# Four edits to a two-block layer: logits over four column strips, the gate exponentials ahead of the row copies, the first transfers in another order, and the first expert's second weights held until the first gathered rows are in

## The reference, cut to what matters

```python
mod = silu(c) @ ada_w + ada_b                 # 1024 x 6144, split in shift1, scale1, gate1, shift2, scale2, gate2
h   = rms_norm(x, norm1_g) * (1 + scale1) + shift1
z   = h @ w_in                                # then RWKV-7 time mix and stick-breaking attention, w_out
h2  = rms_norm(x, norm2_g) * (1 + scale2) + shift2
logits = h2 @ router_w + router_b             # 512 x 32
top_logit, top_idx = top_k(logits, 4); top_gate = softmax(top_logit)
out[token] = sum over its 4 experts e: top_gate * (swiglu(h2 @ w1[e] + b1[e]) @ w2[e] + b2[e])
```

## Time and profile before

| | |
|---|---|
| median of three runs | 2655.41 us (2650.86 to 2656.16) |
| the profiled execution | 2653.22 us, its span 2651.5 us |
| mean granted clock of TensorE in it | 0.964 of full |
| PE busy | 2513.9 us, 95% of the span |
| DVE, ACT, POOL busy | 38%, 15%, 7% |
| moved by transfers | 555.43 MB, mean 209 GB/s |

### The profile page before, as it was taken

One profiled execution on the slowest core, in us unless ns is written; L12 is line 12 of the kernel. 1 busy time (PEld: TensorE's weight loads), 2 busy tenths in 40 slices (PEclk: granted clock), 3 DMA queues, 4 the chain that ended last, 5 costly groups with the idle time before them and its releaser, 6 DMA issues.

```text
span 2651.5 us, 49064 instructions
## 1 busy us (share of the span) xinstructions
PE 2513.9 (95%) x20545; PEld 1407.8 (53%) x20545; DVE 1017.6 (38%) x2012; ACT 406.4 (15%) x797; POOL 196.3 (7%) x256
## 2 busy tenths in 40 slices
PE   4999989796999999999999999699999998999999
PEld 2444777654333344433333444345556544888888
DVE  5563655424322333333222332423145222455551
ACT  2411134412000000000000000101234201111100
POOL 0000000000111111111111111400000000000000
PEclk8999999897999999999999999799999999999999
DMA  7432000105899999999999999750200112121221
GB/s 273 154 127 95 3 2 1 66 0 230 358 421 422 422 422 422 421 422 422 422 422 422 422 422 387 261 184 33 95 33 32 33 32 64 64 96 64 88 66 54
DMA packets 143743, 555.43 MB, mean 209 GB/s; under 512 B 15760, under 2 KB 51632, under 8 KB 94240
## 3 DMA queue, kind: packets, MB, share of 16 engines
q1 hardware_dynamic: 127088, 515.22, 48.9%
q0 software_dynamic: 13984, 36.49, 3.8%
q10 hardware_dynamic: 2576, 2.36, 0.3%
HBM read 537.25 MB, written 16.78 MB: 209 GB/s over the span
## 4 chain that ended last, share of the span: by engine, by line
PE 91%; DVE 4%; ACT 2%; issue 1%; DMA 1%; POOL 1%; SPq 0%; DVEq 0%; ACTq 0%; POOLq 0%
PE psum L2491 25%; PE psum L2082 20%; PE psum L2507 12%; PE psum L2777 10%; PE psum L2806 5%; PE psum L2240 2%; PE psum L2412 2%; PE psum L2696 2%; PE psum L2673 1%; PE psum L2354 1%; PE psum L2380 1%; PE psum L2651 1%; PE psum L2661 1%; PE psum L2070 1%; DVE arena L1305 1%
## 5 line engine op out<-in xcount | busy, mean ns | idle before, releaser
L2491 PE MATMUL psum<-ring,arena 128*32 128x512 f32 x6144 | 668.0, 594 | 10.0 <-DVE arena L1680 6.6
L2491 PEld LDWEIGHTS psum<-ring,arena 128*32 128x32 f32 x6144 | 196.8, 110 | 452.9 <-issue 452.3
L2082 PE MATMUL psum<-hT,ring 128*128 128x512 f32 x752 | 341.4, 611 | 3.4 <-ACT hT L829 3.4
L2507 PE MATMUL psum<-ring,arena 128*32 128x256 f32 x6144 | 337.4, 379 | 2.1 <-DVE arena L1714 2.1
L2507 PEld LDWEIGHTS psum<-ring,arena 128*32 128x32 f32 x6144 | 200.1, 110 | 146.6 <-issue 20.8
L2082 PEld LDWEIGHTS psum<-hT,ring 128*128 128x128 f32 x752 | 145.2, 196 | 182.5 <-issue 181.0
L1680 DVE STREAM_TRANSPOSE arena<-arena 128x768 f32<-128x768 f32 x33 | 32.3, 979 | 512.9 <-PE psum L2491 512.8
L760 POOL DMA_INDIRECT arena<-h_rows,small x102 | 100.1, 981 | 1310.2 <-DVE small L1689 1263.0
L2777 PE MATMUL psum<-ring 128*128 128x256 f32 x704 | 159.1, 379 | 0.5 <-ACT arena L815 0.5
L1014 ACT ACTIVATE arena<-arena 128x768 f32<-128x768 f32 x32 | 27.0, 843 | 823.3 <-DVE arena L1700 823.3
L2777 PEld LDWEIGHTS psum<-ring 128*128 128x128 f32 x704 | 133.7, 190 | 19.1 <-ACT arena L815 0.9
(11 more groups left out here) (391 smaller groups left out, 2590.1 us busy)
## 6 DMA issues: line engine op xcount, KB each, us to landing
ring<-in_exp_w SPq DMA_DIRECT2D x384, 1024.0 KB, 14.3
ring<-in_w_in SPq DMA_DIRECT2D x15, 2048.0 KB, 7.8
ring<-in_ada_w SPq DMA_DIRECT2D x12, 2048.0 KB, 8.1
ring<-in_w_ffn_in SPq DMA_DIRECT2D x22, 1024.0 KB, 7.7
expert_rows<-arena POOLq DMA_DIRECT2D x128, 96.0 KB, 6.0
ring<-in_w_ffn_out SPq DMA_DIRECT2D x8, 1408.0 KB, 6.7
ring<-in_w_out SPq DMA_DIRECT2D x2, 2048.0 KB, 7.9
ring<-in_w_o SPq DMA_DIRECT2D x2, 2048.0 KB, 7.5
```

Of the source, the lines that this page charges most:

```text
L2082: ins = mm(dst, l, r, start=(i == 0), stop=(i == len(parts) - 1))
L2491: ins = mm(bank[s][q * SG:(q + 1) * SG, :], XG[:, k, s * SG:(s + 1) * SG], w[:, q], start=(k == 0), stop=(k == KD - 1))
L2507: ins = mm(bank[3 + s // 2][q * SG:(q + 1) * SG, (s % 2) * 256:(s % 2 + 1) * 256], aT2k[:, s, k // 2, k % 2, :], w2_slot(k)[:, q * 256:(q ...
```

## The change

1. *First transfers.* SP issues `vec` and the positions, then `ada` chunks 0 and 1, then `xT` and `cst`, then `ada` 2 and 3, then the three small matrices, then `lora`, `k` and the rest. DVE begins with `cond` and `ada(0)`, `ada(1)`, and computes the angles between `ada(1)` and `ada(2)`. ACT makes squares and root first and the sines after them. PE sums the first two `ada` chunks ahead of the squares.
2. *Logits.* `router_w[:, k, :]` (32 columns) becomes the loaded weight and 128 tokens of `hT` stream; the four token tiles write to the four strips of 32 partitions of one bank. The result is experts by tokens, so DVE copies it out (128x128), PE transposes it once, and one DVE instruction of 128x128 adds the bias.
3. *Gates.* ACT runs the exponentials before the eight copies of token rows.
4. *Pass count.* Two small instructions over the thresholds take the place of the chain of comparisons.
5. *Second weights.* SP waits for the first gather's 48 counts before it issues w2 of expert 0; B2, the loads of `n_pass` and w1 of expert 1 stand behind that wait in its stream.

```diff
-    keys += [("lg", t) for t in range(NT)] + [("ht", t, i) for t in range(NT) for i in range(2)]
+    keys += [("lg",), ("lgT",)] + [("ht", t, i) for t in range(NT) for i in range(2)]
...
         def _(sp):
-            sp.dma_start(cst[:, :], a["consts"]).then_inc(tables_in, 16)
             sp.dma_start(vec[:, :], a["vecs"]).then_inc(tables_in, 16)
-            sp.dma_start(xT[:, :, :], a["xT"]).then_inc(x_in, 16)
-            sp.dma_start(up_wa[0:64, :], a["decay_up"][0]).then_inc(up_in, 16)
-            sp.dma_start(up_wa[64:128, :], a["iclr_up"][0]).then_inc(up_in, 16)
-            sp.dma_start(up_g, a["gate_up"][0]).then_inc(up_in, 16)
-            sp.dma_start(u_pos[:, :], a["positions"]).then_inc(up_in, 16)
+            sp.dma_start(u_pos[:, :], a["positions"]).then_inc(tables_in, 16)
             for (kind, i), s, after in loads:
+                if (kind, i) == ("ada", 2):
+                    sp.dma_start(xT[:, :, :], a["xT"]).then_inc(x_in, 16)
+                    sp.dma_start(cst[:, :], a["consts"]).then_inc(x_in, 16)
+                elif (kind, i) == ("win", "lora"):
+                    sp.dma_start(up_wa[0:64, :], a["decay_up"][0]).then_inc(up_in, 16)
+                    sp.dma_start(up_wa[64:128, :], a["iclr_up"][0]).then_inc(up_in, 16)
+                    sp.dma_start(up_g, a["gate_up"][0]).then_inc(up_in, 16)
...
             load_w1(0, 0)
+            sp.wait_ge(rows_in, 16 * GROUPS)
             load_w2(0, 0)
...
-            act.wait_ge(x_in, 16)
-            act.wait_ge(tables_dve, 1)
-            act.activation(cos_sin[:, :, :, :].rearrange("p j t f -> p (j t f)"), trig[:, 0:256], ACT.Sin).then_inc(tables_act, 1)
+            act.wait_ge(x_in, 32)
             for k in range(KD):
                 square(k)
             root(0)
+            act.wait_ge(tables_dve, 2)
+            act.activation(cos_sin[:, :, :, :].rearrange("p j t f -> p (j t f)"), trig[:, 0:256], ACT.Sin).then_inc(tables_act, 1)
             scale_shift(0, 0)
...
             scale_shift(1, 24)
+            act.wait_ge(top_ready, 1)
+            act.activation(TOPG, TOPG, ACT.Exp).then_inc(eg_ready, 1)
             for t in range(NT):
                 for i in range(2):
                     take(("ht", t, i), h2_split[:, t, 4 * i:4 * i + 4], ACT.Copy,
...
             act.dma_start(h2_d.rearrange("(t p) n -> p t n", p=P), h2_tok).then_inc(h2_out, 16)
-            act.wait_ge(top_ready, 1)
-            act.activation(TOPG, TOPG, ACT.Exp).then_inc(eg_ready, 1)
...
-            for n in range(4):
-                ada(n)
+            ada(0)
+            ada(1)
+            angles()
+            ada(2)
+            ada(3)
...
-            for t in range(NT):
-                b = plan.bank(("lg", t))
-                dve.wait_ge(filled, plan.at["lg", t] + 1)
-                link_evac(dve.tensor_tensor(LG[:, t, :], bank[b][:, 0:EXPERTS], row("router_b"), ALU.add), ("lg", t))
+            dve.wait_ge(filled, plan.at["lg",] + 1)
+            dve.tensor_copy(logits_T, bank[plan.bank(("lg",))][:, 0:P]).then_inc(evac[plan.bank(("lg",))], 1)
+            dve.wait_ge(filled, plan.at["lgT",] + 1)
+            link_evac(dve.tensor_tensor(LG, bank[plan.bank(("lgT",))][:, 0:P].rearrange("p (t e) -> p t e", t=NT),
+                                        row("router_b")[:, None, :].to_broadcast([P, NT, EXPERTS]), ALU.add), ("lgT",))
...
-            link(dve.tensor_scalar(NPF[:, 1:2], NPF[:, 0:1], CAP + 0.5, 1.0, ALU.is_gt, ALU.add))
-            for n in range(2, MAX_PASS):
-                link(dve.scalar_tensor_tensor(out=NPF[:, 1:2], in0=NPF[:, 0:1], scalar=n * CAP + 0.5, in1=NPF[:, 1:2],
-                                              op0=ALU.is_gt, op1=ALU.add))
-            link(dve.tensor_scalar(NPF[:, 2:3], NPF[:, 1:2], float(EXPERTS), -1.0, ALU.mult, ALU.add))
+            link(dve.tensor_scalar(GTMP[:, 0:MAX_PASS - 1], const("iota", MAX_PASS)[:, 1:MAX_PASS], float(CAP), NPF[:, 0:1], ALU.mult, ALU.is_lt))
+            link(dve.tensor_reduce(NPF[:, 3:4], GTMP[:, 0:MAX_PASS - 1], AX.X, ALU.add))
+            dve.tensor_scalar(NPF[:, 1:2], NPF[:, 3:4], 1.0, None, ALU.add)
+            link(dve.tensor_scalar(NPF[:, 2:3], NPF[:, 3:4], float(EXPERTS), EXPERTS - 1.0, ALU.mult, ALU.add))
...
-            pe.wait_ge(tables_in, 32)
+            pe.wait_ge(x_in, 32)
+            sum_mod(0)
+            sum_mod(1)
             for k in range(KD):
                 sum_square(0, k)
-            for n in range(4):
-                sum_mod(n)
+            sum_mod(2)
+            sum_mod(3)
...
-            for t in range(NT):
-                b = plan.bank(("lg", t))
-                pe.wait_ge(evac[b], plan.turn(("lg", t)))
+            b = plan.bank(("lg",))
+            pe.wait_ge(evac[b], plan.turn(("lg",)))
             for k in range(KD):
                 pe.wait_ge(h_ready, KD + k + 1)
                 for t in range(NT):
-                    ins = mm(bank[plan.bank(("lg", t))][:, 0:EXPERTS], hT[:, k, t * P:(t + 1) * P], router_w[:, k, :],
+                    ins = mm(bank[b][t * EXPERTS:(t + 1) * EXPERTS, 0:P], router_w[:, k, :], hT[:, k, t * P:(t + 1) * P],
                              start=(k == 0), stop=(k == KD - 1))
-                    if k == KD - 1:
-                        ins.then_inc(filled, 1)
+            ins.then_inc(filled, 1)
+            tile_evacuated(pe, ("lg",))
+            turn(("lgT",), [logits_T])
```

More of the change, by code:

```diff
@@ L431, in program @@
         GATE_T = A(26)[0:EXPERTS, :]
+        logits_T = A(27)[:, 0:P]
         B1_ROWS = hflat[:, 0:T]
@@ L1273, in _ @@
             dve.wait_ge(tables_in, 32)
-            dve.wait_ge(up_in, 64)
-            link(dve.tensor_copy(small[:, 120:124], u_pos[:, :]))
-            ang, turns = trig[:, 128:256], trig[:, 256:384]
-            for t in range(NT):
-                ins = dve.tensor_scalar(ang[:, t * 32:(t + 1) * 32], const("inv_freq"), small[:, 120 + t:121 + t], None, ALU.mult)
-            link(ins)
-            link(dve.tensor_scalar(turns, ang, 1.0 / TURN, ROUNDER, ALU.mult, ALU.add))
-            link(dve.tensor_scalar(turns, turns, ROUNDER, None, ALU.subtract))
-            for part in TURN_PARTS:
-                link(dve.scalar_tensor_tensor(out=ang, in0=turns, scalar=-part, in1=ang, op0=ALU.mult, op1=ALU.add))
-            link(dve.tensor_scalar(ang, ang, PI_LOW, -PI_LOW, ALU.min, ALU.max))
-            link(dve.tensor_scalar(trig[:, 0:128], ang, TURN / 4, None, ALU.add))
-            link(dve.tensor_scalar(turns, trig[:, 0:128], TURN / 2, -TURN, ALU.is_gt, ALU.mult))
-            link(dve.tensor_tensor(trig[:, 0:128], trig[:, 0:128], turns, ALU.add))
-            dve.tensor_scalar(trig[:, 0:128], trig[:, 0:128], PI_LOW, -PI_LOW, ALU.min, ALU.max).then_inc(tables_dve, 1)
             dve.tensor_scalar(omka, vec[:, VEC_AT["k_a"]:VEC_AT["k_a"] + 4], -1.0, 1.0, ALU.mult, ALU.add)
@@ L1293, in _, with angles @@
             dve.tensor_tensor(cond, sigc, vec[:, VEC_AT["c"]:VEC_AT["c"] + KD], ALU.mult).then_inc(tables_dve, 1)
-            dve.wait_ge(tables_dve, 2)
+            dve.wait_ge(tables_dve, 1)
+            def angles():
+                dve.wait_ge(x_in, 32)
+                link(dve.tensor_copy(small[:, 120:124], u_pos[:, :]))
+                ang, turns = trig[:, 128:256], trig[:, 256:384]
+                for t in range(NT):
+                    ins = dve.tensor_scalar(ang[:, t * 32:(t + 1) * 32], const("inv_freq"), small[:, 120 + t:121 + t], None, ALU.mult)
+                link(ins)
+                link(dve.tensor_scalar(turns, ang, 1.0 / TURN, ROUNDER, ALU.mult, ALU.add))
+                link(dve.tensor_scalar(turns, turns, ROUNDER, None, ALU.subtract))
+                for part in TURN_PARTS:
+                    link(dve.scalar_tensor_tensor(out=ang, in0=turns, scalar=-part, in1=ang, op0=ALU.mult, op1=ALU.add))
+                link(dve.tensor_scalar(ang, ang, PI_LOW, -PI_LOW, ALU.min, ALU.max))
+                link(dve.tensor_scalar(trig[:, 0:128], ang, TURN / 4, None, ALU.add))
+                link(dve.tensor_scalar(turns, trig[:, 0:128], TURN / 2, -TURN, ALU.is_gt, ALU.mult))
+                link(dve.tensor_tensor(trig[:, 0:128], trig[:, 0:128], turns, ALU.add))
+                dve.tensor_scalar(trig[:, 0:128], trig[:, 0:128], PI_LOW, -PI_LOW, ALU.min, ALU.max).then_inc(tables_dve, 1)
             def ada(n):
@@ L2127, in gates @@
                 if c == 0:
-                    pe.wait_ge(up_in, 64)
+                    pe.wait_ge(up_in, 48)
                     pe.wait_ge(gates_lo, 2)
@@ L2184, in _ @@
             head_sum(0)
-            pe.wait_ge(up_in, 80)
+            pe.wait_ge(up_in, 64)
             pe.wait_ge(inverse_ready, 1)
```

4 lines of the change are left out of this document (1 added, 3 removed).

## The result

| | before | after |
|---|---|---|
| median | 2650.86 us (five runs, 2648.08 to 2656.16) | 2637.10 us (five runs, 2634.99 to 2639.03) |
| ratio after to before | | 0.9942, interval 0.993 to 0.9955 |
| profiled execution, its span | 2653.22, 2651.5 us | 2637.1, 2635.1 us |
| mean granted clock of TensorE | 0.964 | 0.969 |

Two runs of before, taken beside the five of after, joined the three of the forecast. Of the two profiled executions the span is 16.4 us shorter. Three instants divide that difference: the first reciprocal (S), the reciprocal after the first block's residual (R), which begins the routing, and the first expert's first product (F).

A forecast was written before the change was run, and what follows sets the result against it. PE was taken as the bound, with 91% of the chain. Gains of 2.9 (start) and 9.9 (routing) sum to 12.8: 2653.2 becomes 2640.4, and the median, 2.2 above the profiled execution, 2642.5 us; main case 2637 to 2648.

The forecast's parts named there:

- everything from the first product on shifts by the start's 2.9 us: Sign to look for in the trace: all work from PE's first product onward comes 2.9 us earlier.
- Part 1, the start: First transfers reordered: DVE begins sooner, first reciprocal at 40.0 instead of 42.85 us; gain 2.9, bounds 2.3 and 3.6.
- "28.5" and "28.8": At the start, two estimates in us of when the transfers needed before ada(2) have landed; 28.2 was taken.
- Rival (d): The start gives nothing, ada(2) or the angles coming 3 us late: 2645.5 us; inside the main case of chance 0.84.
- Part 2, the logits: Router logits over four strips at 0.11 us per instruction, PE ending at 625.6; first maximum at 626.8, 7.0 us earlier.
- Rival (a): In the logits the strips do not overlap, loads or the four streams serialise: 2649.5 us; chance 0.07.
- Part 3, gates and rows: Exponentials before row copies: store issued at 634.0 instead of 640.28, landed at 641.3; pass count 637.2, 11.2 us earlier.
- Rival (c): PE stays at 1.2 GHz through the counts: gather at 646.1, 2644.5 us; inside the main case of chance 0.84.
- Part 4, the gather: From store landing and POOL's load of the pass number to the gather: at 644.1, 9.9 us earlier, bounds 8 and 11.
- Part 5, the held w2: Holding expert 0's w2 until the first gather leaves 2 us of backlog in the expert loop, cost 0, cover 3 us.
- rival (b): Transfers give out in the expert loop, hidden waits for w1: mild 2647 us, chance 0.06; slow 2659 us, chance 0.03.
- rival (e): Despite held w2 the store takes 9.4 us: gather near 646, 2644.5 us; inside the main case of chance 0.84.

The follow-up runs named there:

- a4_small_late: The changed kernel with the three small matrices (decay_up, iclr_up, gate_up) issued behind the k chunk; 2637.12 us, ratio 0.995 (0.9934 to 0.9965).
- b1_exp_late: The changed kernel with the exponentials again behind the row copies and the store; one execution, gather at R + 30.5, F at R + 37.6, no total time given.

## Where the prediction failed, and where it held

**The steps that failed.** The direction, the stage that carries the gain and what must be held for it came as forecast. The terms of the sum did not. The start was put at 2.9 us and measured 1.3 in the profiled pair, 0.8 over all executions. The routing was put at 9.9 and measured 12.35, above its bounds of 8 to 11. And "everything from the first product on shifts by the start's 2.9 us" put the stretch between S and R at nothing; it was 2.3 us shorter in this pair, by a scatter that reaches 9.8 us over all executions. Together that is 15.9 us at the first expert's product against 12.8: the start gave 1.6 less, the routing 2.45 more and the stretch between them 2.3 more.

**How much of the total was luck.** The medians differ by 13.8 us, close to the forecast 12.9, since the error of the start and that of the routing have opposite signs. Against the 2655.41 us from which the forecast was made the measured median is 18.3 lower; 4.55 of that is only that the median of before fell to 2650.86 with two more runs. The stated 2637 to 2648 does not follow from its terms either: 2641 less 4.5 and 2645 plus 0.8 give 2636.5 to 2646.

**Part 1, the start: mis-sized.** The step that failed is "28.5" and "28.8", the arrival of `ada(2)`, and with it `ada(3)`. Both came from a rate or an arrival of the old order, and took it that bytes cost the same in any order. `ada(0)` began at 10.88 for 9, the angles at 23.91 for 22.8, `ada(2)` at 29.33 for 28.2. `ada(3)` waited 0.32 more where the forecast had no wait, which `a4_small_late` puts down to the small matrices; S was 41.56 for 40.0. Rival (d), the start gives nothing, which lay inside the main case, was nearer to the truth than the 2.9. That the order of large and small rows at the front causes the lower rate is argued from the windows of the first 10 us, not shown: no run changed that alone.

**Part 2, the logits: right, and slightly better.** Taken at 0.11 us each, measured 0.70/8 = 0.088 in the last eight; ended 0.7 us behind ACT's last tile; the first maximum 7.4 us earlier in R's count for 7.0. Rival (a) is excluded by the 5.50 us.

**Part 3, gates and rows: the transposes were mis-sized.** The step that failed is "PE starts to transpose at 626.5 ... and ends at 633.3": it put all 32 transposes at 1.2 GHz, 6.8 us, though the row before has 6.20. They took 5.30, since the clock was up again at 625.7 with about half of them still to do, and they began 0.7 us sooner in R's count. PE was through at R + 16.55 for R + 18.8, and ACT's copies and PE's counts both follow it: the store was issued at R + 17.5 for R + 19.5, and the pass count was done at R + 20.8 for R + 22.7. The table load was misplaced too: the forecast added 1.28 us of it behind the wait for the top four, and the row shows it at 620.84, as soon as ACT was free and 2.6 us before the operand was there. But by the forecast's own times neither the copies nor the gates waited for the exponentials, so that error moved nothing in the sum. The Trainium skill (ScalarE: Activation LUTs, What ACT_TABLE_LOAD costs) adds 1.38 us of drain to a switch. The trace does not agree here: in `b1_exp_late` the load ends at 628.27 + 1.28 = 629.55 and the exponential starts at 629.57. Rival (c) did not happen; the higher clock was back 1.6 us before `pos`.

**Part 4, the gather: the steps right, the sizes off.** Store landing plus POOL's load gave the gather, as worked out: the store took 7.83 for 7.3, then it was 1.96 us to the gather for 2.8. With the store issued 2.0 us early the gather came at R + 27.3 for R + 29.6, hence 12.35 for 9.9.

**Part 5, the held w2: right in effect, wrong in price.** The forecast's 2 us of added backlog cannot be confirmed: the pair shows 1.7, the other runs no difference. It cost nothing, as forecast; rival (b) needed 5.3 and did not come. What failed is rival (e), "the store takes its 9.4 us all the same: gather near 646". That carried over a landing time of the old kernel, where only about 1 MB of w2 was still to move, to a store that is issued some 8 us earlier in R's count. Without the hold the gather comes at R + 37.5, not R + 31.5, and 10.2 of the stage's 12.35 us are lost. The sentence in part 3, "this needs part 5", was the right one, and its price should have been worked from the bytes: 12.6 MB of weights and 2.1 MB of rows at 422 GB/s are 34.8 us, and the first of them moves 1 to 2 us before R, so all of it is over near R + 33. The store, with the smaller packets, ended with the rest at R + 35.0 to 35.6.

## What to carry to other kernels

A transfer that is issued earlier into full queues need not land earlier: here the store got a third of the rate beside the weights and ended when they did, at R + 35, for issues at R + 17 and R + 26. Count the bytes ahead and beside it, and make room by holding what is not wanted soon. When two paths open one step, write both down from one instant, for each combination of edits: here the hold alone gave nothing, the strips alone 2 us, and all together 12. A transfer at the front of the program is better costed by what the first microseconds reach in that order (249 to 274 GB/s here) than by the rate of the old order; why the rate differs is open.

## What was not expected of the hardware

- A 2 MB store on ACT's queue took 7.7 to 8.3 us with w2 held and 18.3 to 18.4 beside the weights on SP's queue, at 414 GB/s in all.
- Beside each other the two queues moved the same number of packets (151 and 150 in 4 us), so the one with the larger packets moved more bytes (1.10 against 0.61 MB).
- A part of the gather took 2.7 us alone and 7.0 us beside w2.
- The program's first 10 us moved 249 to 274 GB/s with one order of the first transfers and 314 to 321 with the other; 422 is reached later.
- In the recurrence, with the same instructions, the granted clock (350 to 414 us) was between 0.84 and 0.97 from one execution to another, and R − S moved by up to 9.8 us.
- PE stayed at 0.50 through 13.8 us of logits without a pause before, and through 5.5 us of them after; in both the clock rose only during the transposes behind them (at 638.4 and 625.7 us).
